# Ranking the third query tile's index scores later on VectorE, in a tile of its own

## The reference, cut to what matters

```python
# branch A: an indexer scores all earlier keys, and each query keeps the best 128
topk = min(TOPK_MAX, s_len // 4)                      # 128
logits = einsum('bthd,bsd->bths', iqb, ik32)          # 8 index heads of 64
score = einsum('bths,bth->bts', relu(logits), iwb) * idx_scale
score = where(causal, score, NEG_BIG)
_, sel = lax.top_k(score, topk)                       # per block of 128 queries
# ... attention over the selected keys alone, with a relative bias

# branch B: gated linear recurrence, 4 heads of 128
b = cumsum(log_f)                                     # inside a chunk
decay = exp(b[t] - b[s])                              # causal
attn = einsum('bhtk,bhsk,bhtsk->bhts', q, k, decay)
o = rms_norm(einsum('bhts,bhsv->bhtv', attn, v) + carried state) * silu(g)

# branch C: latent attention: normed latents, projections, rotary parts,
# softmax attention of 4 heads over 512 keys ("mla" in the kernel)
```

## Time and profile before

| | us |
|---|---|
| median of 3 runs | 1536.9 (1532.97 to 1540.24) |
| the profiled execution's own time | 1537.01 |
| its span in the profile | 1535.2 |
| PE busy | 1412.6 (92%) |
| DVE busy | 949.7 (62%) |
| ACT busy | 540.5 (35%) |
| POOL busy | 54.4 (4%) |
| mean granted TensorE clock | 0.96 of full |

### The profile page before, as it was taken

The page is one execution under the profiler, slowest core; times in us unless marked ns, Lnnn a source line. Parts: engine busy times, 40 slices in busy tenths (PEclk is TensorE's granted clock), DMA queues, the critical chain, the costliest instruction groups (busy, mean ns, idle before and its releaser), DMA issues.

```text
span 1535.2 us, 18934 instructions
## 1 busy us (share of the span) xinstructions
PE 1412.6 (92%) x7110; PEld 1096.0 (71%) x7110; DVE 949.7 (62%) x1608; ACT 540.5 (35%) x896; POOL 54.4 (4%) x45
## 2 busy tenths in 40 slices
PE   5988899999997797997999999999799999988887
PEld 3758798876665465886888888888569854565676
DVE  6249778853767656766445554533497648569772
ACT  5247244432335623333323423432223221224421
POOL 0000000000005400000000000000000001000000
PEclk9999999999998898998999999899899899989999
DMA  5203111222221213541344434122521212520001
GB/s 228 81 28 110 56 56 56 73 83 91 81 81 44 76 49 107 202 161 58 112 158 147 161 143 160 57 100 90 151 72 52 83 55 82 178 97 1 1 1 55
DMA packets 40170, 141.04 MB, mean 92 GB/s; under 512 B 13072, under 2 KB 17552, under 8 KB 27536
## 3 DMA queue, kind: packets, MB, share of 16 engines
q1 hardware_dynamic: 34896, 131.05, 24.2%
q10 hardware_dynamic: 5184, 8.78, 1.6%
HBM read 128.94 MB, written 8.39 MB: 89 GB/s over the span
## 4 chain that ended last, share of the span: by engine, by line
PE 80%; DVE 14%; ACT 3%; issue 2%; DMA 1%; SPq 0%; ACTq 0%; DVEq 0%
PE turn L714 25%; PE score L714 18%; PE score L699 8%; PE sum L714 8%; PE sum L699 6%; PE turn L939 2%; DVE ring_r L1899 2%; PE score L852 1%; PE sum L1282 1%; DVE stat L1970 1%; DVE work L1971 1%; DVE work L1899 1%; PE sum L1164 1%; PE score L1164 1%; PE turn L836 1%
## 5 line engine op out<-in xcount | busy, mean ns | idle before, releaser
L1899 DVE TENSOR_TENSOR ring_r<-ring,heads_r 128x1024 fp32r<-128x1024 f32 (+3 forms) x161 | 186.1, 1156 | 193.9 <-ACT heads_r L1390 190.7
L1390 ACT ACTIVATE heads_r<-ring 128x1024 fp32r<-128x1024 f32 (+3 forms) x161 | 161.8, 1005 | 248.2 <-DMA ring<-wstream 120.4
L714 PE MATMUL score<-h_sb_r,heads_r 128*128 128x512 f32 x400 | 161.5, 404 | 0.0
L714 PE MATMUL turn<-tiles_r,heads_r 128*128 128x512 f32 x368 | 145.1, 394 | 0.0
L714 PE MATMUL turn<-h_sb_r,heads_r 128*128 128x512 f32 x336 | 132.5, 394 | 8.1 <-DVE ring_r L1899 8.1
L714 PE MATMUL turn<-wide_r,heads_r 128*128 128x512 f32 x312 | 122.1, 391 | 0.0
L714 PE MATMUL turn<-wide_r,ring_r 128*128 128x512 f32 x312 | 121.9, 391 | 0.0
L714 PE MATMUL score<-x_sb_r,heads_r 128*128 128x512 f32 x248 | 107.3, 433 | 10.1 <-DVE ring_r L1899 7.7
L714 PE MATMUL score<-x_sb_r,ring_r 128*128 128x512 f32 x248 | 101.2, 408 | 0.0
L714 PEld LDWEIGHTS score<-h_sb_r,heads_r 128*128 128x128 f32 x400 | 78.8, 197 | 14.8 <-DVE tiles_r L1899 0.2
L714 PEld LDWEIGHTS turn<-tiles_r,heads_r 128*128 128x128 f32 x368 | 70.4, 191 | 14.6
(11 more groups left out here) (400 smaller groups left out, 2895.7 us busy)
## 6 DMA issues: line engine op xcount, KB each, us to landing
ring<-wstream SPq DMA_DIRECT2D x95, 1024.0 KB, 5.0
ring<-wstream SPq DMA_DIRECT2D x16, 704.0 KB, 4.3
ring<-gated SPq DMA_DIRECT2D x6, 1024.0 KB, 7.1
gated<-tiles ACTq DMA_DIRECT2D x18, 256.0 KB, 2.0
x_sb<-xT SPq DMA_DIRECT2D x4, 512.0 KB, 5.7
x_sb<-xT ACTq DMA_DIRECT2D x1, 2048.0 KB, 8.1
outT<-x_sb SPq DMA_DIRECT2D x1, 2048.0 KB, 6.3
ring<-wstream SPq DMA_DIRECT2D x3, 512.0 KB, 3.5
```

The source lines that it names most:

```text
L714: return pe.matmul(out, a, w, **k) if moving else pe.matmul(out, w, a, **k)
L1390: step(act.activation(head_piece(p), chunk(name)[:, c:c + cols], ACT.Identity), f"head {p}")
L1899: step(dve.tensor_tensor(out, a, b, op), name)
```

## The change

The ranking of tile 2 gets its own tile `ranked2` of 384 columns. Its 16 take_tops and its `choose` leave the ranking stage. The clamp, the four scans and the rests of places `rank 3` and `rank 4` stay there and now follow `choose(1)` directly. Six take_tops stand behind the rests of place `latent 1`, ahead of the four gatings `rec oT n`; ten and `choose(2)` stand behind these, ahead of the wait for `trig` and the rotary parts.

```diff
+    ranked2 = sb("ranked2", 3 * P)
...
-    RANKED = [None, INDEX[1], INDEX[2], TL[:, 4, :]]
+    RANKED = [None, INDEX[1], ranked2[:, :], TL[:, 4, :]]
...
             choose(1)
-            for i in range(TOPK // 8):
-                take_top(2)
-                if i == 7:
-                    dve.wait_ge(act_step, at("rec floor"))
-                    stt(f4, f4, LOG_FLOOR, w0, ALU.max, ALU.add)
-                    for h in range(4):
-                        bt = TL[:, 5 + h, :]
-                        step(dve.tensor_tensor_scan(bt, con("reset"), bt, 0.0, ALU.mult, ALU.add))
-                if i in (11, 13):
-                    beside(f"rank {i // 2 - 2}")
-            choose(2)
+            beside("rank 3")
+            dve.wait_ge(act_step, at("rec floor"))
+            stt(f4, f4, LOG_FLOOR, w0, ALU.max, ALU.add)
+            for h in range(4):
+                bt = TL[:, 5 + h, :]
+                step(dve.tensor_tensor_scan(bt, con("reset"), bt, 0.0, ALU.mult, ALU.add))
+                if h == 1:
+                    beside("rank 4")
             beside("rank 5")
             beside("rank 6")
...
             weight_rests(upto=pieces_through(PLACE["latent 1"]))
+            for _ in range(6):
+                take_top(2)
             for n in range(NT):
...
                 stt(TL[:, 9:13, n * P:(n + 1) * P], U[m % 2][:, :].rearrange("p (j t) -> p j t", j=4), sm("g_ob")[:, 0:1],
                     TL[:, 18:22, n * P:(n + 1) * P], ALU.mult, ALU.mult, f"rec oT {n}", turn_done)
+            for _ in range(6, TOPK // 8):
+                take_top(2)
+            choose(2)
             dve.wait_ge(act_step, at("trig"))
```

## The result

The changed kernel takes 1526.5 us (median of 8 runs, 1518.4 to 1531.2) against 1535.3 us (8 runs, 1532.7 to 1540.2) before, a ratio of 0.9934, 95% interval 0.9916 to 0.9951. That is 8.8 us by medians, and faster by more than 0.5% at the ratio's centre, not over the whole interval. The interval spans 7.5 to 12.9 us.

The account below looks back on a forecast made before the run. DVE's order in the ranking stage was taken to make PE wait. The stop, 6.03 us, and the low clock behind it, 2.96, made 8.99: 1537.0 - 9.0 = 1528.0 us, range 1524.5 to 1533 for 8 in 10.

Parts of the forecast that it names:

- The stop and its cause: Ranking stage: PE waits 5.9 us for a rest queued behind tile 2's take_tops; removing the stop gives 6.03 us.
- The clock's share: First proj1g tile: without the stop it runs in 5.44 us in place of 8.40, giving 2.96 us.
- only the stop goes: Rival, first proj1g tile: PE stays at the low clock for part of it; 1531.0 us, chance 0.12.
- The four rests: Ranking stage: DVE's rests for the four proj1g tiles all end before PE wants them, so none binds.
- The new wait of DVE: Ranking stage, first rest: DVE, free at 142.86, waits about 8 us for the ACT head ending at 150.79.
- The recurrence passes it on: Recurrence: its start moves with PE's tiles and PE has no idle time there, so the whole 8.99 us passes.
- The latent stage costs nothing: Latent stage: DVE's idle time hides the moved take_tops and choose; cost 0, up to 20.4 us without that cover.
- the rival on the other side: Latent stage turns into the bound, slower if a take_top takes above 2.27 us; 1540.7 us at 2.5, chance 0.05.
- Given back later: Rival: the recurrence or a later exchange has a bound not moving with PE; 9 us lost, 1537.0 us, chance 0.08.

Follow-up runs that it names:

- the control: The changed kernel run once more with no edit, against the kernel before: median 1524.8 us, ratio 0.9922.
- rests moved, ranking kept: The kernel before with only the four proj1g rests moved forward among the take_tops, tile 2's ranking left in its stage: 1527.6 us, ratio 0.9951.
- all 16 ahead: The changed kernel with all 16 take_tops and the choose of tile 2 ahead of the four gatings: 1541.6 us, ratio 1.0037 to before.
- tile 2 not ranked: The changed kernel with the 16 take_tops of tile 2 left out and the choose kept: 1526.6 us, ratio 0.9930 to before.

## Why the prediction was right

It said 1528.0 us, 9.0 less than before; the medians differ by 8.8. That the two agree within 0.2 us is luck, since the interval reaches from 7.5 to 12.9 us; what carries the account are the marks in the traces. The measured 1526.5 lies 1.5 us below the forecast mainly because the kernel before has a median of 1535.3 over eight runs, where the prediction started from 1537.0.

- *The stop and its cause.* Said: PE waits for a rest that stands behind take_tops although its head is ready. The wait is gone with the change, and goes as well when only the rests move: it was order.
- *The clock's share.* Said 2.96 us if it comes back whole. The first tile took 5.46 in place of 8.40: 2.94. In the control and in the profiled executions of "rests moved, ranking kept", "all 16 ahead" and "tile 2 not ranked" it took 5.46 or 5.47 as well, so the rival "only the stop goes" is out. The prediction's doubt, that the price of a stop differs from run to run, shows elsewhere: the kernel before with its drains moved pays 2.3 us for the low clock behind its stop at this tile, in place of 2.96.
- *The four rests.* Said to end at 152.0, 158.2, 163.5 and 169.8; they end at 152.4, 158.5, 163.9 and 170.2. The new wait of DVE, said to be 8 us, is 8.15.
- *The recurrence passes it on.* Said 8.99; 8.64 at its start and 8.60 at its end. Of the missing 0.35, 0.32 was there before the repaired place: the last rows1 matmul starts at 160.76 in place of 160.44, and 0.22 of that is there already at 144.20, where PE comes out of the stop before (143.98 before).
- *The latent stage costs nothing.* Said: 1.46 us spare ahead of the gatings; measured 1.42. Said: 5.8 us spare ahead of `kpe`; the last rotary instruction ends at 364.47 and the turn starts at 370.29, 5.8 later. Leaving the work out gained nothing (187.58 us in place of 187.62 from the recurrence to `kpe`), and putting it all ahead of the gatings cost the predicted stop (11.1 us against 11.4). A take_top on the new tile takes 1.25 us, so the rival on the other side is out with its condition.
- *Given back later.* Between `kpe` and the output stage the first profile gives back 2.4 us and the control 1.8, with no new wait, as time at the low clock. The same stretch is as long, 221.0 us, in a kernel with VectorE's old order, so the rival's mechanism, a bound that doesn't move with PE, isn't what the traces show; whether a part of the lead is given back more often with the change stays open.

What the prediction put no price on is how much the low clock in other stages differs between executions of one program. The two profiles of the changed kernel at hand, 1531.05 and 1524.8 us, lie 6.0 and 12.2 under the one of before; the lead at marks ahead of `mla` is the steadier reading: 8.6 us in the one, and 9.9 in the control, of which 1.3 come from less time at the low clock behind the stop of 4.0 us.

## What to carry to other kernels

When a busy engine makes another wait, look first at which of its instructions the other waits for and when that one's input was ready; here four instructions of 1.2 us held the time, and moving them gave what moving 20 us of work gave. The amount matters once the stops ahead are gone: repair in the order in which they bind, and expect a repair behind another bound to measure as zero (1.0002 here). Work put into another engine's idle time is free up to the length of the gap ahead of the next instruction that somebody waits for, not up to the idle time of the stage: 7.5 us into 8.96 cost nothing, 20.4 us cost 11 to 17, in a stage with 24 us idle.

## What the runs showed of the hardware

A stop of PE does not have one price. Behind 4.0 us of idle time the clock over 140 to 151 us was 0.69 in one execution and 0.84 in another of the same program; behind 3.0 us, in the one execution with such a stop, it was 1.00 over 159 to 175 us. Around a wait of 1.8 us in the mla stage, with stops of 0.42 and 0.85 us in the 3 us ahead of it, it was 0.77 and 0.89 over 15 us; with that wait removed and the two others left it was 1.00 over 340 to 385 us. Two profiles of one program differ by 15 us in the time at 1.2 GHz and by 6.3 us in the span, and its runs by 12.8 us (1518.4 to 1531.2). A change of a few us in such a kernel is better read from the distance between marks in the trace than from a handful of times, and of marks close behind the changed place: 220 us further on the same lead of 8.60 us read 6.25.
